# Hybrid encoder step: earlier start of three weight-block sums, a later one of the fourth, and another operand order in the block stages

## What is computed

```
def finish_layer(x, a, b, ga, gb, w_a, w_b, w_o, g1, b1, w_up, w_down, g2, b2):
    mix = (ga * (a @ w_a) + gb * (b @ w_b)) @ w_o
    x = layer_norm(ALPHA * x + mix, g1, b1)
    h = jnp.square(jax.nn.relu(x @ w_up)) @ w_down
    return layer_norm(ALPHA * x + h, g2, b2)
```

## Time and profile before

| | us |
|---|---|
| median of 3 runs | 2154.99 (2145.44 to 2157.51) |
| profiled execution | 2145.24 |
| its span, first to last instruction | 2143.4 |
| PE busy | 2118.8 (99%) |
| DVE busy | 1471.3 (69%) |
| ACT busy | 1230.3 (57%) |
| POOL busy | 65.1 (3%) |
| DMA | 399.27 MB, mean 186 GB/s |

### The profile page before, as it was taken

One profiled execution on the slowest core, in us unless ns is written; L12 is line 12 of the kernel. 1 busy time (PEld: TensorE's weight loads), 2 busy tenths in 40 slices (PEclk: granted clock), 3 DMA queues, 4 the chain that ended last, 5 costly groups with the idle time before them and its releaser, 6 DMA issues.

```text
span 2143.4 us, 38213 instructions
## 1 busy us (share of the span) xinstructions
PE 2118.8 (99%) x15004; PEld 1936.0 (90%) x15004; DVE 1471.3 (69%) x2336; ACT 1230.3 (57%) x2493; POOL 65.1 (3%) x100
## 2 busy tenths in 40 slices
PE   9999999999989999999999999999999899999998
PEld 7998889999979898989889888899999798989897
DVE  6757777677869356665667577786768693566646
ACT  4457776696525356656234677766865253656561
POOL 1100000001000000000001000000010000000000
PEclk9999999999999999999999999999999999999999
DMA  7877562577894345454368765525778932454541
GB/s 256 240 279 258 210 234 82 159 238 213 222 323 104 103 130 172 151 166 139 108 189 245 289 249 202 205 88 177 223 203 255 294 105 93 139 171 152 168 148 69
DMA packets 100866, 399.27 MB, mean 186 GB/s; under 512 B 15272, under 2 KB 16936, under 8 KB 87600
## 3 DMA queue, kind: packets, MB, share of 16 engines
q1 hardware_dynamic: 67904, 191.55, 26.3%
q0 software_dynamic: 7936, 92.28, 17.2%
q10 hardware_dynamic: 24848, 112.99, 14.7%
HBM read 367.42 MB, written 118.23 MB: 227 GB/s over the span
## 4 chain that ended last, share of the span: by engine, by line
PE 96%; DMA 2%; ACT 1%; DVE 1%; issue 0%; SPq 0%; DVEq 0%; ACTq 0%
PE PS L826 9%; PE PS L828 9%; PE PS L827 9%; PE PS L1047 6%; PE PS L1049 6%; PE PS L1048 6%; PE PS L916 5%; PE PS L917 5%; PE PS L915 5%; PE PS L860 4%; PE PS L861 4%; PE PS L859 4%; PE PS L986 3%; PE PS L987 3%; PE PS L985 3%; PE PS L1175 2%
## 5 line engine op out<-in xcount | busy, mean ns | idle before, releaser
L826 PE MATMUL PS<-xt_hi,w_hi 128*128 128x320 f32 x1184 | 382.1, 323 | 0.3
L828 PE MATMUL PS<-xt_hi,w_lo 128*128 128x320 f32 x1184 | 365.7, 309 | 0.0
L827 PE MATMUL PS<-xt_lo,w_hi 128*128 128x320 f32 x1184 | 365.5, 309 | 0.0
L2539 DVE TENSOR_TENSOR w_lo<-w_raw,w_hi 128x1024 fp32r<-128x1024 f32 x146 | 177.3, 1222 | 162.0 <-ACT w_hi L1577 160.4
L2546 DVE TENSOR_TENSOR w_lo<-w_raw,w_hi 128x1024 fp32r<-128x1024 f32 (+1 forms) x176 | 199.2, 1138 | 114.9 <-ACT w_hi L1593 114.6
L1577 ACT ACTIVATE w_hi<-w_raw 128x1024 fp32r<-128x1024 f32 x146 | 153.3, 1059 | 189.6 <-PE PS L1049 155.8
L826 PEld LDWEIGHTS PS<-xt_hi,w_hi 128*128 128x128 f32 x1184 | 222.7, 188 | 5.4 <-issue 4.3
L827 PEld LDWEIGHTS PS<-xt_lo,w_hi 128*128 128x128 f32 x1184 | 223.0, 188 | 0.1
L828 PEld LDWEIGHTS PS<-xt_hi,w_lo 128*128 128x128 f32 x1184 | 222.2, 188 | 0.0
L1593 ACT ACTIVATE w_hi<-w_raw 128x1024 fp32r<-128x1024 f32 (+1 forms) x176 | 172.2, 984 | 86.1 <-PE PS L987 66.3
L1047 PE MATMUL PS<-w_hi,act_a_hi 128*128 128x512 f32 x480 | 189.7, 395 | 13.2 <-DVE rows L3005 13.2
(11 more groups left out here) (391 smaller groups left out, 5088.2 us busy)
## 6 DMA issues: line engine op xcount, KB each, us to landing
w_raw<-in_weights SPq DMA_DIRECT2D x186, 512.0 KB, 4.6
kc<-in_k_cache ACTq DMA_DIRECT2D x32, 1024.0 KB, 7.5
vc<-in_v_cache ACTq DMA_DIRECT2D x16, 2048.0 KB, 8.7
w_raw<-up_sums SPq DMA_DIRECT2D x112, 256.0 KB, 2.8
up_sums<-in_up_blocks POOLq DMA_DIRECT2D x24, 1024.0 KB, 10.1
w_raw<-in_up_blocks SPq DMA_DIRECT2D x84, 256.0 KB, 2.8
down_sums<-in_down_blocks POOLq DMA_DIRECT2D x16, 1024.0 KB, 10.6
w_raw<-in_down_blocks SPq DMA_DIRECT2D x32, 512.0 KB, 3.5
```

Of the source, the lines that this page charges most:

```text
L826: mm(out, wh, hi[:, k, c], start=(k == 0), stop=False)
L827: mm(out, wh, lo[:, k, c], start=False, stop=False)
L828: last = mm(out, wl, hi[:, k, c], start=False, stop=(k == KT - 1))
L2539: v.tensor_tensor(w_lo[slot][:], raw[:, raw_of(s, n)[0], :], w_hi[slot][:].bitcast(F32), ALU.subtract)\
```

## The change

GpSimd's wait ahead of down 1 is now for the last cached product of the layer's last head (`dec_pv`), and up 3 gets a wait of its own, for the first weight chunk of the plain down stage. The other jobs keep their order. In the block stages the operand that serves a single row tile moves from the sixth place to the second; the loads, TensorE's calls, and the counts and places of ScalarE's and VectorE's pieces follow.

```
-            for o, (kind, b) in enumerate((("a", 0), ("s", 0), ("s", 1), ("a", 2), ("s", 2), ("a", 1), ("a", 3),
+            for o, (kind, b) in enumerate((("a", 0), ("a", 1), ("s", 0), ("s", 1), ("a", 2), ("s", 2), ("a", 3),
                                            ("s", 3))):
...
                 elif (kind, part) == ("down", 1):
-                    pool.wait_ge(w_ready[0], nth(l, AT_SWA, 2) + 1)
+                    pool.wait_ge(dec_pv, 2 * HEADS * (l + 1))
+                elif (kind, part) == ("up", 3):
+                    pool.wait_ge(w_ready[0], down_at(l, 0) + 1)
...
                             (4, tile(0, 4), lambda: pe.wait_ge(c11_taken, q + 1))], True, even_ready)
-                operand(1, [(6, sum_tile(1, 0), lambda: pe.wait_ge(p5_copied, q + 1)),
+                operand(1, [(5, tile(0, 4), lambda: pe.wait_ge(c21_taken, q + 1))], True, lambda u: None)
+                operand(2, [(6, sum_tile(1, 0), lambda: pe.wait_ge(p5_copied, q + 1)),
                             (7, sum_tile(1, 1), lambda: pe.wait_ge(up_taken, 2 * q + 2))], True,
                         lambda u: u % 2 == 0 and pe.wait_ge(s_lo_ready, 5 * d + 1 + u // 2))
-                operand(2, [(0, sum_tile(2, 0), seeds(1)), (1, sum_tile(2, 1), None)], False,
+                operand(3, [(0, sum_tile(2, 0), seeds(1)), (1, sum_tile(2, 1), None)], False,
                         lambda u: u == 0 and pe.wait_ge(s_lo_ready, 5 * d + 3))
-                operand(3, [(2, tile(1, 0), None), (3, tile(1, 2), None), (4, tile(1, 4), None)], False, odd_ready)
-                operand(4, [(0, sum_tile(3, 0), seeds(2)), (1, sum_tile(3, 1), None)], False,
+                operand(4, [(2, tile(1, 0), None), (3, tile(1, 2), None), (4, tile(1, 4), None)], False, odd_ready)
+                operand(5, [(0, sum_tile(3, 0), seeds(2)), (1, sum_tile(3, 1), None)], False,
                         lambda u: u == 0 and pe.wait_ge(s_lo_ready, 5 * d + 4))
-                operand(5, [(5, tile(0, 4), lambda: pe.wait_ge(c21_taken, q + 1))], True, lambda u: None)
...
                 if which == 3:
-                    act.wait_ge(ring_done, ring_block(l, part) + 6)
+                    act.wait_ge(ring_done, ring_block(l, part) + 8)
...
-                act.wait_ge(ring_done, g + (2, 6, 10)[i])
+                act.wait_ge(ring_done, g + (2, 8, 12)[i])
...
                 sum_high(l, part, 2)
-                highs(5, 8)
+                highs(5, 11)
                 sum_high(l, part, 3)
-                highs(8, 9)
+                highs(11, 12)
                 block_seed(l, part, 1)
-                highs(9, 11)
                 sum_high(l, part, 4)
-                highs(11, 14)
+                highs(12, 15)
                 block_seed(l, part, 2)
-                highs(14, 20)
+                highs(15, 20)
...
-                dve.wait_ge(ring_done, g + (4, 4, 8, 8, 10, 14, 14, 16, 16)[i])
+                dve.wait_ge(ring_done, g + (6, 6, 10, 10, 12, 14, 14, 16, 16)[i])
...
                 sum_low(l, part, 2)
-                lows(5, 6)
+                lows(5, 9)
                 takes(0, 1)
-                lows(6, 8)
+                lows(9, 11)
                 sum_low(l, part, 3)
-                lows(8, 11)
+                lows(11, 12)
                 sum_low(l, part, 4)
+                lows(12, 13)
                 takes(2, 3)
-                lows(11, 13)
-                lows(13, 14)
+                lows(13, 16)
                 takes(4)
-                lows(14, 17)
+                lows(16, 17)
                 takes(5, 6)
```

## The result

| | before | after |
|---|---|---|
| median of 20 runs | 2150.46 us (2142.79 to 2157.53) | 2154.67 us (2150.28 to 2165.28) |
| profiled execution | 2145.24 | 2153.42 |
| its span | 2143.4 | 2151.6 |
| mean granted clock | 0.996 | 0.995 |

What follows compares the result with a forecast made beforehand. TensorE, busy 99% of the span, was taken as the bound. 2145.2 - 17.0 (norm stage) + 13.0 (gates) = 2141, plus half the execution gap gave 2146 us; forecast's own range 2136 to 2156, 8 in 10 within 2128 to 2164.

Steps and rivals of the forecast that it cites:

- The bound and the norm stage: TensorE 99% busy; two L1047 waits plus slow clock hold 17.6 us; gain 17.0, bounds 10 and 17.6.
- VectorE's own chain: Norm stage: rounding and first take release TensorE near 620.2, where it arrives at 620.0; late about 0.3 us a layer.
- Up 3 beside the plain down stage: Plain down stage: four chunks held ahead, 27 us, cover landings; nothing lost, or 0 to 2 us if up 3 slips.
- the block order: Block stages: same 216 matmuls reordered, sixth ring chunk's margin 1.1 us; cost 0, bounds 0 and 4 blocks x 1 us.
- The gates: Branch A's pairs: ScalarE's gate loads land late beside up 2; 6.5 us a layer, 13 us in both.
- The deadlines: Branch A's pairs: TensorE stops if a first gate lands over 6.0 us after issue, a second over about 7.3.
- a step's last third: Branch A beside up 2: last third of each sum step called quiet, so two of six later loads taken as late.
- the slower rival: Also *Slower*: branch A, more gates caught, from 28 us of new waits; up to +22, 2158 to 2167; chance 0.15.
- the bound of 39 us: Branch A: upper bound of the gates' cost, all twelve late (6 x 3.9 + 6 x 2.6).
- Half the gap: Whole kernel: profiled execution lies 9.8 us under the median of three runs; half added, 2141 to 2146 us.
- The gates fit: Rival, branch A: 0 to 6 us of waits; 2128 to 2134 by profiled execution, up to 2142 by median; chance 0.30.

Runs made afterwards that it cites:

- late up 3 alone: Kernel before with only up 3 held until the plain down stage; old sum start and block order kept: 2129.8 us, ratio 0.9901.
- up 2 held: Changed kernel with up 2 held until the window attention's cache has landed, near 430: 2134.8 us, ratio 0.9927.
- without the gates' loads: Changed kernel without branch A's eight stored-gate loads a layer, the sigmoid taking what the buffers hold: 2130.9 us, ratio 0.9918.
- the cache's loads by SyncE: Changed kernel with the two loads of the window's cache issued by SyncE instead of ScalarE, a few us earlier: 2148.5 us, ratio 0.9998.
- the kernel without the two causes: Changed kernel with branch A's stored-gate loads left out and the window's cache loaded by SyncE: 2127.8 us, ratio 0.9901.
- the two new waits alone: Kernel before with GpSimd's two new waits (down 1 and up 3), without the new block order: 2156.6 us, ratio 1.0035.

## Why the prediction was right or wrong

**The bound and the norm stage: right.** The two waits at L1047 and the slow stretches behind them went, 17.6 us, and late up 3 alone brought 20 by the medians. The chunks' landing fell to 4.4 us, as the forecast of about 5 had it. The cause, up 3's copies, is shown from both sides: held alone it frees the stage, put back alone it brings 6.5 us of waits. Down 2's end, which the prediction named beside them, has a smaller share. No wait is left in the changed kernel's trace, so VectorE's own chain (0.3 us a layer in the forecast) costs at most some tenths.

**Up 3 beside the plain down stage, and the block order: right.** No wait stands in either; the block order alone measures 1.000.

**The gates: the right mechanism, one term near, one term missing.** The deadlines held up. In the changed kernel second gates that landed after 11.0 and 12.2 us should stop TensorE for 3.7 and 4.9 us over the 7.3 and did for 3.04 and 4.31; a first gate with 6.9 us should for 0.9 over the 6.0 and did for 1.15, and one with 5.8 us brought no seed wait. With up 2 held, a first gate with 8.6 us should for 2.6 and did for 2.83. One reading behind the term was off: a step's last third is not quiet. In the double accumulate from 500.57 to 515.46 the packets of GpSimd's queue still take 71% of the DMA engines' time between 511 and 513, and only then fall to 5%. The forecast had 13 us of waits from four late gates; the trace has 8.5 from three. What the sum left out is the slow clock behind them: two of the four stretches, 6.8 us at half speed, 3.4 us lost. It stood in the rows of before, and I priced it for the gain and for the slower rival but not for my own forecast. That was the first fault. That 8.5 + 1.2 + 3.4 = 13.1 is the 13 of the sum is an accident: the waits were over-counted and the clock left out. Nor is the term firm: without the gates' loads the median falls by 24 us, and another execution (the cache's loads by SyncE) had 20.4 us of seed waits.

**The second wait behind branch A: the step that failed.** The prediction said of ScalarE's queue only what it loads into gates. It never asked what the other transfers of ScalarE's queue become beside a running sum, and the queue's own issue times were in the trace: the issue of the cached values took 1.38 us before, four times the usual 0.34. It took 6.67 and 4.89 us after. The wait for the swapped queries (7.3 us) and its two slow stretches (10.2 us long, 8.7 us of TensorE's work in them, 4.4 lost) are 11.7 us that the sum put at nothing; the bound of 39 us was set for gates alone. Forecast 2141 by the profiled execution, plus 11.7, is 2152.7; measured 2153.4. That this still lies within 0.5% of the kernel before is no merit of the sum: an unpriced term of 11.7 us turned a gain into a loss and was just small enough for the band.

**From the profiled execution to the median.** Half the gap, 5 us, was fair: over 20 runs before's median is 5.2 us above its profiled execution. The changed kernel's is 1.3 us above its own.

**The rivals.** *The gates fit* did not come true here, but its time, 2128 to 2134, is about what late up 3 alone (2129.8) and the kernel without the two causes (2127.8) gave. *Slower* had the right sign, in part with another cause: not more gates were late in the trace (three), and of the 25.8 us of new costs, just under its point of 28, 18.0 are waits, 7.3 of them behind the cache's issue.

## What to carry to other kernels

A transfer stream moved out of one stage's way is moved into another's: list every transfer of every queue in the new place, with its deadline, and the issues themselves too, since an issue that is slow already stops its engine when the DMA engines are busy. When a change has an earlier and a later half, try each alone; here the later half held all of the gain (0.990) and the earlier one turned it into a loss (1.003). A wait of some 3 us on a full TensorE costs more than itself, for it can be followed by a stretch at half speed.

## What was not expected of the hardware

The issue of a transfer can block its engine for up to 7 us. In the kernel before, the 256 KB load issued right behind the 512 KB one took 1.38 and 1.57 us to issue. Beside a sum it took 6.67 and 4.89 us in the changed kernel, 7.20 and 2.96 without the gates' loads, and 7.28 and 7.10 on SyncE's queue, while the gates' loads just ahead of it kept to 0.33 to 0.35 us. That it follows a load of many small rows (64 values each) suggests that pieces of that load pile up ahead of it; no run here changed the rows' size, so this is not shown.

TensorE's waits brought 1.2 GHz stretches at lengths of 2.76 to 4.56 us too, not only at the 6 to 7 us of before. But not each time: waits of 2.83 us (up 2 held), 3.08 us (the cache's loads by SyncE) and 3.77 us (the two new waits alone, before 1513.21) have none. And the kernels without a contended wait repeat far better: 2128.4 to 2131.8 us for late up 3 alone, against 2140.9 to 2156.6 for the kernel before in the same job.
